# Last stage: loads in another order and exponentials grouped; prompt attention: both heads turned together

## The chip, the cores and the metric

The kernel runs on one core of a Trainium2 chip. The metric is the device time of one execution in microseconds. TensorE (PE in the rows) multiplies and transposes, VectorE (DVE) and ScalarE (ACT) work on what it leaves in PSUM, GpSimd (POOL) takes elementwise work on SBUF, and SyncE (SP) issues nearly all transfers between DRAM and SBUF. Each engine runs its own instructions in order; they meet through semaphores.

## The reference

One step of a two-layer decoder, for a prompt of 512 positions and for 8 samples of 4 new positions each over a past of 1024. All is float32. Layer A is a dilated sliding-window attention in three groups merged by their softmax denominators. Layer B has three branches with keys and values of their own: compressed blocks, the best selected blocks, a window.

```python
# layer A: for each group g, then merged over g by softmax of lse
s = q @ k.T * SCALE;  s = where(band, s, -inf)
o, lse = softmax(s) @ v, logsumexp(s)
# layer B, each sample (pool of pages through a page table)
hid   = silu(w1 . flatten(32 rows) + pe)         # compressed keys and values: w2 . hid
o_cmp = softmax(q . k_cmp) @ v_cmp               # its probabilities choose the 16 blocks
o_sel = softmax(q . k of the chosen blocks) @ v
o_win = softmax(q . k of the window) @ v
y = x + ((g0*o_cmp + g1*o_sel + g2*o_win) * silu(z)) @ w_out
```

## The kernel before

The program is a row of stages with a barrier between them: layer A (normalise, project, attention of the prompt, attention of the samples, output projection), then layer B the same way. Within a stage the order of each engine's work is written out by hand, and two stages are touched by the change.

**Attention of the prompt, layer A** (`attend_a_stage`). Sixteen steps: four query tiles by four pairs of heads. For each pair TensorE computes the scores of both heads (L585, L589) into four PSUM banks; VectorE adds the mask, writes the result to SBUF and keeps the least value (L669 to L675, "mask"); ScalarE takes the exponential and its sum (L642); VectorE inverts the sum (L680); GpSimd multiplies (L655); TensorE turns the 128 x 768 probabilities of one head with six transposes (L602); VectorE copies four of the six tiles to SBUF (L558) and ScalarE two (L560); TensorE multiplies by the values (L617). The steps are pipelined: in step s TensorE does the scores of s, the transposes of the first head of s-2, the values of s-3, and the transposes of the second head of s-2. There is one pair of banks for turned probabilities, so the second head's transposes wait for both copies of the first head. VectorE's order in a step is: mask of both heads, copy of the first head, one inversion, copy of the second head, the other inversion, and after every fourth step the product of a finished tile with the gate (L695, "merge"). The output of two tiles alternates between two banks.

**Samples, layer B** (`sample_b_stage`, the last stage). Two pieces of work are interleaved by a running number g, the quarter. The first piece compresses the pages of the 8 samples one after the other: transposes of pages (L1375), copies by VectorE and ScalarE, 16 products in a row into one bank (L1390), a silu on ScalarE (L1456), a small product (L1405). It takes 8 quarters a sample for 64 turns of pages, 72 quarters in all. The second piece is the attention of a pair of samples, 16 quarters each (a position i from 0 to 15), beginning at g = 20: transposes of keys of the window and of the selected pages (L2115, six units for i = 0 to 5), scores (L2130), the compressed scores (L2151, i = 4), the exponentials of the window (L2284, i = 3), of the compressed branch (L2290, i = 4) and of the selected branch (L2294, i = 10), the transposes of the probabilities (i = 12), the product with the values (L2174 to L2183, i = 14). Transposes of pages and of keys take turns on two PSUM banks, so each waits until the one before last has been copied. From g = 72 on the last pair's attention is interleaved with the output projection, 17 pieces (L2208): first the eight that use the second half of the output weights, then those of the first half. These weights overwrite the compression's weights and a page buffer.

The order of SP's queue is that of its issues in the code: `load_cmp(n)` loads the compressed branch's pages of sample n (8 transfers, L1550, two buffers), `load_keys(pair, units)` the keys of a pair (L2056 window, L2059 selected pages), `load_values(pair)` the values (L2069, L2070), which wait until the pair before has used its own. The page's number is read from a table in SBUF first (L2034). Behind the third pair's loads come the kept input (L2084) and the output weights (L2089 second half, L2092 first half).

ScalarE holds one table of functions; where the next function is in another table, the compiler puts an ACT_TABLE_LOAD in front. Exponential and silu are in different tables; copy and square do not ask for a load in this program.

Of the kernel before, what the change touches and what calls it, by code (L numbers as in the profile page):

```python
# [528 lines left out]
def attend_a_stage(S, QK, V, Z, T, oT, ring, tables):  # L529


    nc = S.nc
# [6 lines left out]
    with ExitStack() as ctx:  # L539
# [10 lines left out]
        SA, SB, TRA, TRB, OB = S.banks[0:2], S.banks[2:4], S.banks[4], S.banks[5], S.banks[6:8]  # L550
        ZB = [TRA, TRB, OB[0], OB[1]]

        def copy_out(engine, v, by_vector):
            engine.wait_ge(s_tr, v + 1)
            if v >= 4:
                engine.wait_ge(s_pv, v // 2 - 1)
            if by_vector:
                nc.vector.tensor_copy(pT[:, v % 4, 0:TILES, :], TRA[:, :].rearrange("p (c q) -> p c q", q=P)).then_inc(s_ev[0], 1)  # L558
            else:
                nc.scalar.activation(pT[:, v % 4, TILES:, :], TRB[:, 0:2 * P].rearrange("p (c q) -> p c q", q=P),  # L560
                                     ACT.Copy).then_inc(s_ev[1], 1)

        with S.block() as block:
# [8 lines left out]
            def _(pe):  # L572
# [20 lines left out]
                def turn(v):  # L593
                    pe.wait_ge(s_p, v + 1)
                    if v:
                        pe.wait_ge(s_ev[0], v)
                        pe.wait_ge(s_ev[1], v)
                    else:
                        pe.wait_ge(s_zc, 2)
                    for c in range(CH):  # L600
                        bank, at = (TRA, c) if c < TILES else (TRB, c - TILES)
                        ins = nc.tensor.transpose(bank[:, at * P:(at + 1) * P], probs[:, v % SLOTS, c * P:(c + 1) * P], ident)  # L602
                    ins.then_inc(s_tr, 1)

                def values(s):
                    t, j = divmod(s, HP)
                    for e in range(2):
                        pe.wait_ge(s_ev[e], 2 * (s + 1))
                    if s == 0:
                        pe.wait_ge(s_zc, TILES)  # L610
                    if j == 0 and t >= 2:
                        pe.wait_ge(s_fin, t - 1)
                    for c in range(CH):
                        g, kt = (0, c) if c < TILES else (c - TILES + 1, t)
                        for e in range(2):
                            h = 2 * j + e
                            ins = nc.tensor.matmul(OB[t % 2][e * DH:(e + 1) * DH, j * P:(j + 1) * P], V[:, g, kt, h * DH:(h + 1) * DH],  # L617
                                                   pT[:, (2 * s + e) % 4, c, :], start=(c == 0), stop=(c == CH - 1), skip_group_check=True)
# [39 lines left out]
            def _(dve):  # L658
# [4 lines left out]
                def mask(v):  # L663
# [3 lines left out]
                    if v >= SLOTS:  # L667
                        dve.wait_ge(s_tr, v - SLOTS + 1)
# [1886 lines left out]
```

## Time and profile before

| | us |
|---|---|
| median of 3 runs | 1436.12 (1435.59 to 1440.30) |
| the profiled execution | 1431.16 |
| its span, first to last instruction | 1429.4 |
| prompt attention of layer A | about 345 to 447 |
| last stage | about 1082 to 1429 |

Positions below are microseconds from the start of the span. A row of a timeline gives start, duration, engine, line, operation, what it writes and reads, and in brackets the time for which the engine stood idle before and what ended that. TensorE is busy for 89% of the span, the others for a third or less, but busy matmuls are partly waiting in the pipeline; the places where TensorE is idle say more.

### The profile page before, as it was taken

The page shows a single profiled execution, that of the slowest core. Times are in us where ns is not written, and L with a number is a line of the kernel's source. Part 1 is how long each engine was busy: PE and PEld are TensorE (multiplying, and loading weights), DVE is VectorE, ACT ScalarE, POOL GpSimd, SP SyncE. Part 2 cuts the span into 40 slices and gives each one's busy share as a digit, 9 for nine tenths or more (in the row PEclk, how much of TensorE's full clock was granted, in tenths as well). Part 3 has the DMA queues.
Part 4 walks back from the last instruction along what each step waited for, and adds up shares of the span by engine and source line. Part 5 has one row for each costly group of instructions (what it writes and reads, how often), then busy time and mean ns, then how long its engine had stood idle before and what let it go on. Part 6 is the DMA issues. An engine that isn't in the chain of part 4 may idle for free. (4 is left out here: it accounts for less than half of the span.)

```text
span 1429.4 us, 21435 instructions
## 1 busy us (share of the span) xinstructions
PE 1272.5 (89%) x7792; PEld 803.2 (56%) x7792; DVE 489.9 (34%) x1378; ACT 404.9 (28%) x958; POOL 362.3 (25%) x443
## 2 busy tenths in 40 slices
PE   3999999998886898889999998889998799999399
PEld 2576675764665762444444647655566567667144
DVE  1333332001675321223322102456773244534132
ACT  4111111112442210131211111456663244543100
POOL 1455553001774000026523100345441000000000
PEclk9999999999998998989999797689999899999699
DMA  6143333343104995132223531696454564553711
GB/s 221 55 179 119 127 149 149 129 177 79 37 2 113 278 265 141 36 143 89 88 88 97 208 63 30 218 336 238 148 207 157 154 203 141 181 182 109 180 24 63
DMA packets 88075, 200.26 MB, mean 140 GB/s; under 512 B 10131, under 2 KB 39235, under 8 KB 86563
## 3 DMA queue, kind: packets, MB, share of 16 engines
q1 hardware_dynamic: 87970, 198.89, 43.6%
q8 instruction: 63, 1.03, 0.3%
q14 instruction: 42, 0.34, 0.1%
HBM read 186.08 MB, written 75.37 MB: 183 GB/s over the span
## 5 line engine op out<-in xcount | busy, mean ns | idle before, releaser
L437 PE MATMUL bank<-la_region,la_hT 128*128 128x512 f32 x640 | 283.7, 600 | 1.6 <-PEq L162 1.6
L437 PEld LDWEIGHTS bank<-la_region,la_hT 128*128 128x128 f32 x640 | 165.7, 263 | 103.9 <-issue 61.9
L1183 PE MATMUL bank<-lb_region,lb_oT 128*128 128x512 f32 (+2 forms) x528 | 214.3, 568 | 1.6 <-PEq L162 1.6
L1183 PEld LDWEIGHTS bank<-lb_region,lb_oT 128*128 128x128 f32 (+1 forms) x528 | 99.4, 206 | 104.5 <-issue 104.2
L1390 PE MATMUL bank<-cs_chunks_turned,lb_region 128*128 128x252 f32 x512 | 126.3, 385 | 8.1 <-ACT cs_hidden L1456 8.0
L655 POOL TENSOR_SCALAR aa_probs<-aa_probs,aa_rec 128x768 f32<-128x768 f32 x32 | 70.2, 2205 | 137.8 <-DVE aa_rec L680 137.8
L1390 PEld LDWEIGHTS bank<-cs_chunks_turned,lb_region 128*128 128x128 f32 x512 | 92.1, 193 | 19.6 <-issue 7.2
L1759 POOL TENSOR_SCALAR ab_probs<-ab_probs,ab_rec,lb_gates 128x128 f32<-128x128 f32 (+3 forms) x128 | 75.9, 608 | 50.1 <-DVE ab_rec L1786 50.1
L2208 PE MATMUL bank<-lb_region,lb_oT 128*128 128x512 f32 x128 | 58.6, 610 | 22.6 <-DMA lb_region<-in_b_w_out 22.6
L1729 ACT ACTIVATE ab_probs<-ab_probs,ab_low 128x128 f32<-128x128 f32 (+3 forms) x128 | 70.4, 551 | 26.1 <-DVE ab_low L1780 25.9
L1445 DVE COPY cs_chunks_turned<-bank 64x512 f32<-64x512 f32 x64 | 43.7, 683 | 85.5 <-PE bank L1375 85.0
L485 POOL TENSOR_TENSOR pa_swapped<-pa_normed,pa_tables 128x256 f32<-128x256 f32 (+1 forms) x60 | 50.2, 855 | 77.3 <-DVE pa_normed L504 77.3
L1447 ACT ACTIVATE cs_chunks_turned<-bank 64x512 f32<-64x512 f32 x64 | 37.9, 593 | 95.7 <-PE bank L1375 95.0
L1684 PEld LDWEIGHTS bank<-consts,ab_probs 128*128 128x128 f32 (+1 forms) x384 | 43.9, 144 | 33.8 <-issue 19.5
L1684 PE MATMUL bank<-consts,ab_probs 128*128 128x128 f32 (+1 forms) x384 | 60.2, 298 | 2.5 <-POOL ab_probs L1752 1.5
L456 ACT ACTIVATE pa_squares<-bank 128x512 f32<-128x512 f32 (+1 forms) x30 | 16.0, 533 | 163.0 <-PE bank L437 155.4
L1487 POOL TENSOR_SCALAR cs_ms<-cs_ss 63x4 f32<-63x4 f32 x8 | 1.5, 186 | 229.3 <-DVE cs_ss L1498 229.3
L1780 DVE CUSTOM_DVE_ANT_0 ab_probs<-bank,consts 128x128 f32<-128x128 f32 (+3 forms) x128 | 56.1, 483 | 6.6 <-PE bank L1660 6.3
L2208 PEld LDWEIGHTS bank<-lb_region,lb_oT 128*128 128x128 f32 x128 | 24.2, 195 | 51.4 <-issue 50.3
L475 POOL TENSOR_TENSOR pa_rstd<-pa_mean_square,consts 128x8 f32<-128x8 f32 (+1 forms) x30 | 51.0, 1699 | 2.5
L1211 ACT ACTIVATE pb_squares<-bank 128x256 f32<-128x256 f32 (+3 forms) x25 | 10.6, 424 | 131.6 <-PE bank L1183 126.3
L1660 PE MATMUL bank<-lb_kT,lb_qp 64*128 64x128 f32 (+3 forms) x256 | 44.4, 484 | 3.0 <-DVE ab_low L1780 2.2
(312 smaller groups left out, 1807.0 us busy)
## 6 DMA issues: line engine op xcount, KB each, us to landing
la_region<-in_a_w_in SPq DMA_DIRECT2D x10, 2048.0 KB, 8.0
sb_sel_pages<-in_cache_nsa_paged SPq DMA_DIRECT2D x128, 128.0 KB, 2.4
out_new_dil_s<-in_cache_dil SPq DMA_DIRECT2D x8, 2032.0 KB, 12.5
lb_region<-in_b_w_in SPq DMA_DIRECT2D x7, 2048.0 KB, 7.8
sa_cache<-in_cache_dil SPq DMA_DIRECT2D x9, 1024.0 KB, 13.4
x<-in_cache_nsa_paged SPq DMA_DIRECT2D x32, 256.0 KB, 3.7
lb_region<-in_cache_nsa_paged SPq DMA_DIRECT2D x32, 256.0 KB, 3.9
sb_win_rows<-in_cache_nsa_win SPq DMA_DIRECT2D x16, 512.0 KB, 4.2
```

The lines of the kernel that those rows point to most:

```text
L437: ins = nc.tensor.matmul(U[u.v % 4][:, :], permuted(hT[:, k, :], u.g, u.t), W[:, u.c % 2, k, :], start=(k == 0), stop=(k == KC - 1))
L475: nc.gpsimd.tensor_tensor(rstd[:, i % 2, 0:u.H], ms[:, 0:u.H], S.const("half_power")[:, 0:u.H], ALU.pow).then_inc(s_rstd, 1)
L485: nc.gpsimd.tensor_tensor(o3[:, :, lo:lo + HALF], n3[:, :, HALF - lo:DH - lo], tab, ALU.mult).then_inc(s_sw, 1)
L655: nc.gpsimd.tensor_scalar(p, p, rec[:, v % SLOTS:v % SLOTS + 1], None, ALU.mult).then_inc(s_p, 1)
L1183: ins = nc.tensor.matmul(U[u.v % 3][0:u.R, 0:n], hT[:, k, u.t * P:u.t * P + u.R], W[:, u.c % 2, k, 0:n], start=(k == 0), stop=(k == KC - 1))
L1390: ins = nc.tensor.matmul(self.hid_bank[:, 0:KVH * nb], self.w1[:, kv, off, mm, :], self.chunksT[:, y % 2, :, mm, off:off + nb], start=(rm ...
L1660: nc.tensor.matmul(SC[u.i % 4][:, at:at + x.N], q, KT[part, x.br - 1, x.j, 0:x.N], start=True, stop=True, skip_group_check=True).then_inc( ...
L1684: ins = nc.tensor.transpose(TR[k2][0:x.rows, at:at + P], src[:, c * P:c * P + x.rows], ident)
L1729: nc.scalar.activation(row(u), row(u), ACT.Exp, bias=low[:, p, i:i + 1], scale=-1.0, accum_out=den[:, p, i:i + 1]).then_inc(s_e, 1)
L1759: nc.gpsimd.tensor_scalar(row(u), row(u), rec[:, x.b % 2, u.i:u.i + 1], gate, ALU.mult, ALU.mult).then_inc(s_p, 1)
L1780: nc.vector.tensor_tensor_reduce(row(u), SC[u.i % 4][:, at:at + x.N], S.const("causal")[:, (TILES - 1 - x.t) * P:], -SCALE, 3e38, ALU.add, ...
L2208: ins = nc.tensor.matmul(bank[:, :], oT[:, 4 * part + k, t * P:(t + 1) * P], W_out[:, 4 * part + k, half * 512:half * 512 + 512], start=(k ...
```

## The change

In the prompt attention the twelve transposes of a pair now stand together, with one signal at their end; VectorE has a bank for each head, ScalarE copies the rest of both heads at once (128 x 512), and the output has one bank for all tiles. VectorE's mask of the second head stands behind the copy of the first head's transposes, the inversions at the end of a step, and the merge at the beginning of a step instead of at its end. In the last stage the third sample's compressed pages are loaded behind three of six units of the first pair's keys, the fourth sample's ahead of the first pair's values, and the second half of the output weights ahead of the last pair's values. The exponential of the window moves from i = 3 to i = 4, next to that of the compressed branch, and behind each group of exponentials a silu of one element is added for as long as pages are compressed.

```diff
@@ attend_a_stage
-        SA, SB, TRA, TRB, OB = S.banks[0:2], S.banks[2:4], S.banks[4], S.banks[5], S.banks[6:8]
+        SA, SB, TRA, TRB, OB = S.banks[0:2], S.banks[2:4], S.banks[4:6], S.banks[6], S.banks[7]
...
+        def copy_first(s, e):
+            nc.vector.wait_ge(s_tr, s + 1)
+            if s >= 2:
+                nc.vector.wait_ge(s_pv, s - 1)
+            nc.vector.tensor_copy(pT[:, (2 * s + e) % 4, 0:TILES, :], TRA[e][:, :].rearrange("p (c q) -> p c q", q=P)).then_inc(s_ev[0], 1)
+
+        def copy_last(s):
+            nc.scalar.wait_ge(s_tr, s + 1)
...
+            nc.scalar.activation(pT[:, i:i + 2, TILES:, :], TRB[:, :].rearrange("p (e c q) -> p e c q", e=2, q=P),
+                                 ACT.Copy).then_inc(s_ev[1], 1)
...
+                def turn(s):
+                    if s:
+                        pe.wait_ge(s_ev[0], 2 * s)
+                        pe.wait_ge(s_ev[1], s)
...
+                    for e in range(2):
+                        v = 2 * s + e
+                        pe.wait_ge(s_p, v + 1)
+                        for c in range(CH):
+                            bank, at = (TRA[e], c) if c < TILES else (TRB, 2 * e + c - TILES)
+                            ins = nc.tensor.transpose(bank[:, at * P:(at + 1) * P], probs[:, v % SLOTS, c * P:(c + 1) * P], ident)
                     ins.then_inc(s_tr, 1)
...
                     if 2 <= s < NP + 2:
-                        turn(2 * (s - 2))
+                        turn(s - 2)
                     if s >= 3:
                         values(s - 3)
-                    if 2 <= s < NP + 2:
-                        turn(2 * (s - 2) + 1)
...
                 for s in range(NP + 4):
-                    if s < NP:
-                        mask(2 * s)
-                        mask(2 * s + 1)
+                    if s >= HP + 3 and (s - 3) % HP == 0:
+                        merge((s - 3) // HP - 1)
                     for e in range(2):
+                        if s < NP:
+                            mask(2 * s + e)
                         if 2 <= s < NP + 2:
-                            copy_out(dve, 2 * (s - 2) + e, True)
+                            copy_first(s - 2, e)
+                    for e in range(2):
                         if s < NP:
                             invert(2 * s + e)
@@ sample_b_stage, SP
                 load_cmp(1)
-                load_keys(0, range(NU))
+                load_keys(0, range(0, 3))
                 load_cmp(2)
+                load_keys(0, range(3, NU))
+                load_cmp(3)
                 load_values(0)
-                load_cmp(3)
...
-                    load_values(pair + 1)
-                    if pair == NPAIR - 2:
                         sp.wait_ge(C.m["tr"], 8 * NB)
                         for k2 in range(2):
                             sp.dma_start(W_out[k2 * DH:(k2 + 1) * DH, 4:8, :], w[1, k2]).then_inc(s_w[1], 16)
+                    load_values(pair + 1)
+                    if pair == NPAIR - 2:
                         sp.wait_ge(C.m["hm"], 2 * NB)
@@ sample_b_stage, ScalarE
-                    if i == 3:
+                    if i == 4:
                         act.wait_ge(m["lwin"], pair + 1)
                         nc.scalar.activation(pwin[:, :], pwin[:, :], ACT.Exp, bias=low[:, 2:3], scale=SCALE,
                                              accum_out=den[:, 2:3]).then_inc(m["ewin"], 1)
-                    if i == 4:
                         act.wait_ge(m["lcmp"], pair + 1)
...
+                        if g < C.quarters:
+                            nc.scalar.activation(idle[:, 1:2], idle[:, 0:1], ACT.Silu)
                     if i == 10:
...
+                        if g < C.quarters:
+                            nc.scalar.activation(idle[:, 1:2], idle[:, 0:1], ACT.Silu)
```

How this stands on the engines, at three places. Line numbers of the changed kernel are 5 to 13 higher.

TensorE, one step in the middle of the prompt attention (bank: PSUM; aa_probs: probabilities; aa_probs_turned: the same turned; la_v: values), before:

```order
L585 MATMUL bank<-la_qk 128x512 x2
L589 MATMUL bank<-la_qk 128x128 x4
L602 MATMUL bank<-consts,aa_probs 128x128 x6
L617 MATMUL bank<-aa_probs_turned,la_v 64x128 x12
L602 MATMUL bank<-consts,aa_probs 128x128 x6
```

The same step in the changed kernel:

```order
L590 MATMUL bank<-la_qk 128x512 x2
L594 MATMUL bank<-la_qk 128x128 x4
L609 MATMUL bank<-consts,aa_probs 128x128 x12
L624 MATMUL bank<-aa_probs_turned,la_v 64x128 x12
```

The second head's six transposes have moved from behind the values to ahead of them.

ScalarE, from the copy of the fourth key unit (i = 3) to the page copy of i = 5 in a pair that runs beside the compression (cs_hidden: the silu; sb_p_win, sb_p_cmp: exponentials; cs_chunks_turned, sb_keys_turned: copies that free a bank), before:

```order
L2264 ACTIVATE sb_keys_turned<-bank 128x512
L2284 ACT_TABLE_LOAD
L2284 ACTIVATE sb_p_win,sb_den<-sb_p_win,sb_low 128x544
L1456 ACT_TABLE_LOAD
L1456 ACTIVATE cs_hidden<-bank,lb_pe_hidden 128x4x63
L1447 ACTIVATE cs_chunks_turned<-bank 64x512
L2264 ACTIVATE sb_keys_turned<-bank 128x512
L2290 ACT_TABLE_LOAD
L2290 ACTIVATE sb_p_cmp,sb_den<-bank,sb_low 128x63
L1447 ACTIVATE cs_chunks_turned<-bank 64x512
```

The same stretch in the changed kernel:

```order
L2272 ACTIVATE sb_keys_turned<-bank 128x512
L1462 ACTIVATE cs_hidden<-bank,lb_pe_hidden 128x4x63
L1453 ACTIVATE cs_chunks_turned<-bank 64x512
L2272 ACTIVATE sb_keys_turned<-bank 128x512
L2293 ACT_TABLE_LOAD
L2293 ACTIVATE sb_p_win,sb_den<-sb_p_win,sb_low 128x544
L2298 ACTIVATE sb_p_cmp,sb_den<-bank,sb_low 128x63
L2301 ACT_TABLE_LOAD
L2301 ACTIVATE sb_idle<-sb_idle 1x1
L1453 ACTIVATE cs_chunks_turned<-bank 64x512
```

Two of three loads are left, and both stand between the second key copy and the page copy of i = 5.

SP, from the kept input on (x<-scratch_x), in two pieces, before; between them stand the other 17 transfers of the last pair's values:

```order
L2084 DMA x<-scratch_x 128x4096 [waits cs_tr]
L2034 TENSOR_LOAD page_table [waits sb_pv]
L2034 ISA x2
L2069 ISA
L2069 DMA sb_sel_pages<-in_cache_nsa_paged 128x256
```

```order
L2070 DMA sb_win_rows<-in_cache_nsa_win 128x4x256
L2089 DMA lb_region<-in_b_w_out 64x4x1024 [waits cs_tr]
L2089 DMA lb_region<-in_b_w_out 64x4x1024
L2092 DMA lb_region<-in_b_w_out 64x4x1024 [waits cs_hm]
L2092 DMA lb_region<-in_b_w_out 64x4x1024
```

In the changed kernel:

```order
L2092 DMA x<-scratch_x 128x4096 [waits cs_tr]
L2095 DMA lb_region<-in_b_w_out 64x4x1024 [waits cs_tr]
L2095 DMA lb_region<-in_b_w_out 64x4x1024
L2041 TENSOR_LOAD page_table [waits sb_pv]
L2041 ISA x2
L2076 ISA
L2076 DMA sb_sel_pages<-in_cache_nsa_paged 128x256
```

The two transfers of the weights' second half have moved ahead of the wait for the third pair's product (sb_pv); those of the first half stay behind the values.

## Rows read from the trace of the kernel before

**Rows 1.** First line of the page.

```profile
span 1429.4 us, 21435 instructions
```

**Rows 2.** Timeline of TensorE in the last stage: start, duration, what, idle before.

```profile
1114.09 1.87 PE L1390 MATMUL bank<-cs_chunks_turned,lb_region 128*128 128x252 f32 x8
1126.39 1.11 PE L1375 MATMUL bank<-consts,x 128*128 128x128 f32 x4 [10.44 <-DMA x<-in_cache_nsa_paged]
1127.29 2.77 PE L1390 MATMUL bank<-cs_chunks_turned,lb_region 128*128 128x252 f32 x8
...
1156.59 1.11 PE L1375 MATMUL bank<-consts,lb_region 128*128 128x128 f32 x4 [2.52 <-DMA lb_region<-in_cache_nsa_paged]
...
1183.63 0.60 PE L1375 MATMUL bank<-consts,x 128*128 128x128 f32 x4
...
1245.14 0.60 PE L1375 MATMUL bank<-consts,x 128*128 128x128 f32 x4
...
1308.47 1.94 PE L1390 MATMUL bank<-cs_chunks_turned,lb_region 128*128 128x252 f32 x8 [1.66 <-ACT cs_hidden L1456]
...
1354.63 5.25 PE L2208 MATMUL bank<-lb_region,lb_oT 128*128 128x512 f32 x8 [22.63 <-DMA lb_region<-in_b_w_out]
...
1378.75 13.98 PE L2208 MATMUL bank<-lb_region,lb_oT 128*128 128x512 f32 x32
```

**Rows 3.** List of waits, last stage: waiter, releaser, total us, times, longest.

```profile
PE bank L1390 <- ACT cs_hidden L1456: 8.0, 6, 1.9
```

**Rows 4.** Timeline of SP's issues in the last stage; duration covers all xN transfers.

```profile
1095.18 17.04 SPq L2059 DMA_DIRECT2D sb_sel_pages<-in_cache_nsa_paged  x16
1113.01 10.12 SPq L1550 DMA_DIRECT2D x<-in_cache_nsa_paged  x8
...
1163.98 10.08 SPq L1550 DMA_DIRECT2D x<-in_cache_nsa_paged  x8
...
1183.76 9.62 SPq L1550 DMA_DIRECT2D lb_region<-in_cache_nsa_paged  x8
1198.47 8.49 SPq L2069 DMA_DIRECT2D sb_sel_pages<-in_cache_nsa_paged  x8
...
1228.47 9.72 SPq L1550 DMA_DIRECT2D x<-in_cache_nsa_paged  x8
...
1320.59 8.45 SPq L2069 DMA_DIRECT2D sb_sel_pages<-in_cache_nsa_paged  x8
...
1339.17 1.29 SPq L2089 DMA_DIRECT2D lb_region<-in_b_w_out  x2
```

**Rows 5.** SP's own list of waits, last stage (L2183: end of a pair's product).

```profile
SPq L2034 <- PE bank L2183: 26.4, 3, 20.8
```

**Rows 6.** DMA issues, 1290 to 1360: KB each, median us from issue to landing.

```profile
lb_region<-in_b_w_out SPq DMA_DIRECT2D x4, 1024.0 KB, 16.8
```

**Rows 7.** Timeline of all engines about i = 4 of the second pair.

```profile
1218.61 1.28 ACT L1456 ACT_TABLE_LOAD   x1
...
1219.91 0.47 ACT L1456 ACTIVATE cs_hidden<-bank,lb_pe_hidden 128x252 f32<-128x252 f32 x1
...
1220.52 1.09 PE L1390 MATMUL bank<-cs_chunks_turned,lb_region 128*128 128x252 f32 x4 [1.86 <-ACT cs_hidden L1456]
...
1226.50 0.60 PE L2115 MATMUL bank<-consts,sb_sel_pages 128*128 128x128 f32 x4
```

**Rows 8.** Timeline of all engines, one step of the prompt attention.

```profile
373.63 0.85 PE L602 MATMUL bank<-consts,aa_probs 128*128 128x128 f32 x6 [0.93 <-DVE aa_probs_turned L558]
...
374.41 1.25 PE L585 MATMUL bank<-la_qk 64*128 64x512 f32 x4
...
376.15 0.69 DVE L669 CUSTOM_DVE_ANT_0 aa_probs<-bank,la_region 128x512 f32<-128x512 f32 x1 [0.88 <-PE bank L589]
...
378.51 0.69 DVE L558 COPY aa_probs_turned<-bank 128x512 f32<-128x512 f32 x1
...
379.30 0.85 PE L602 MATMUL bank<-consts,aa_probs 128*128 128x128 f32 x6 [0.93 <-DVE aa_probs_turned L558]
```

More of the change, by code:

```diff
@@ L549, in attend_a_stage @@
         s_ev = [S.sem("aa_copied_by_vector"), S.sem("aa_copied_by_scalar")]
-        SA, SB, TRA, TRB, OB = S.banks[0:2], S.banks[2:4], S.banks[4], S.banks[5], S.banks[6:8]
[L551 to L561, printed above, removed]
+        SA, SB, TRA, TRB, OB = S.banks[0:2], S.banks[2:4], S.banks[4:6], S.banks[6], S.banks[7]
+        ZB = [TRA[0], TRB, TRA[1], OB]
+        def copy_first(s, e):
[5 more added lines that the diff above has]
+            nc.scalar.wait_ge(s_tr, s + 1)
+            if s >= 2:
+                nc.scalar.wait_ge(s_pv, s - 1)
+            i = 2 * s % 4
+            nc.scalar.activation(pT[:, i:i + 2, TILES:, :], TRB[:, :].rearrange("p (e c q) -> p e c q", e=2, q=P),
+                                 ACT.Copy).then_inc(s_ev[1], 1)
         with S.block() as block:
@@ L591, in scores @@
                     ins.then_inc(s_sc, 1)
[L593 to L597, printed above, removed]
-                    else:
[L599 to L602, printed above, removed]
+                def turn(s):
+                    if s:
+                        pe.wait_ge(s_ev[0], 2 * s)
+                        pe.wait_ge(s_ev[1], s)
+                    else:
+                        pe.wait_ge(s_zc, 3)
+                    for e in range(2):
[4 more added lines that the diff above has]
+                            ins = nc.tensor.transpose(bank[:, at * P:(at + 1) * P], probs[:, v % SLOTS, c * P:(c + 1) * P], ident)
                     ins.then_inc(s_tr, 1)
@@ L606, in values @@
                     t, j = divmod(s, HP)
-                    for e in range(2):
-                        pe.wait_ge(s_ev[e], 2 * (s + 1))
+                    pe.wait_ge(s_ev[0], 2 * (s + 1))
+                    pe.wait_ge(s_ev[1], s + 1)
                     if s == 0:
                         pe.wait_ge(s_zc, TILES)
-                    if j == 0 and t >= 2:
-                        pe.wait_ge(s_fin, t - 1)
+                    if j == 0 and t:
+                        pe.wait_ge(s_fin, t)
                     for c in range(CH):
@@ L1955, in sample_b_stage @@
         y_rows = sb("sample_rows", [NS, D])
+        idle = sb("idle", [1, 2])
         s_k = [S.sem(f"sb_keys{u}") for u in range(NU)]
@@ L2267, in _ @@
             def _(act):
+                act.wait_ge(m["idle"], 1)
                 for g in range(NPOS):
@@ L2307, in _ @@
                 link = linker(dve, m["link"])
+                nc.vector.memset(idle[:, 0:1], 0.0).then_inc(m["idle"], 1)
                 link(nc.vector.memset(bmask[:, :], 0.0))
```

21 lines of the change are left out of this document (10 added, 11 removed).

## The prediction

> **What bounds the kernel now.** I read the page's first line, then the list of waits of the last stage, then SP's row of DMA issues against TensorE's timeline there, ScalarE around one pair of samples, and last one step of the prompt attention. The span is 1429.4 us [rows 1]; that execution took 1431.16, so 1.8 lies around the span, and it is 5.0 below the median of the runs, 1436.12. The sum is made against 1431.16 and then moved to the median.
>
> The last stage runs from about 1082 to the end. TensorE is its clock, with four kinds of holes. It waits 10.44 for the third sample's compressed pages, 2.52 for the fourth's, and 22.63 for the output weights [rows 2], and six times for the silu, 8.0 in all [rows 3]. After a long hole it restarts slowly: four transposes in 1.11 where 0.60 is usual and the products behind them in 2.77 instead of 1.87, eight output matmuls in 5.25 where 32 later ones take 13.98, so 3.50 per eight [rows 2].
>
> What the DMA waits rest on is SP. Sixteen selected pages cost it 17.04, so 1.07 each; eight compressed pages 9.6 to 10.1 [rows 4]. Between its first load and the second pair's values it is released by nothing it had waited for: its wait for the output product comes only three times, 20.8 of the 26.4 in the last [rows 5]. Until 1193.4 (1183.76 + 9.62) SP issues without a break. A load moved forward there moves another back.
>
> **Output weights.** Now they stand behind the last pair's values, which wait for the third pair's output product: SP starts at 1320.59, is through at 1339.17, and TensorE, ready at 1354.63 - 22.63 = 1332.0, starts at 1354.63. In the new order the second half (the one used first) waits only for the last page transposes, done before 1306.8 (1308.47 - 1.66) [rows 2]. With the 7.5 found below that is 1299.3; 1.3 to issue, and at most 16.8 to land, which was the time with all four pieces in flight [rows 6]: 1317.4, and TensorE comes at 1324.5. The wait goes whole, with the slow first projection: -22.63 - (5.25 - 3.50) = -24.4. Its cover is 7 us. What is late next would be the first half: values from 1313.1, 18.6 long, then 1.3 + 16.8 gives 1349.8. The ninth projection needs it; it now starts at 1378.75 + 3 x 3.5 = 1389.2, 34.6 after the first, so 1324.5 + 34.6 - 1.75 = 1357.3. Again 7 us of cover. If a piece took twice as long, some 10 us would return; nothing makes it better than -24.4.
>
> **Compressed pages.** After 4 selected pages instead of 16 SP begins the third sample's load at 1095.18 + 4.3 + 0.8 (the gap to 1113.01 now) = 1100.3, ends at 1110.4, and the data is there 3.3 later (1126.39 - 1123.13): 1113.7. TensorE comes at 1114.09 + 1.87 = 1115.96 [rows 2, 4]. So 10.4 goes, and 1.3 of slow restart (0.5 and 0.9 by the rows above, a little of it overlapped). Next, 0.8 + 12.8 of selected pages and 0.8 + 10.1: the fourth sample's last issue is at 1134.9, landed at 1138.2, wanted at 1156.59 - 2.52 - 11.7 = 1142.4. That wait goes too, with as much slow restart: TensorE is 15.6 early, 14.5 after the new wait of the next part.
>
> But then comes the fifth sample. Exactly the same loads stand ahead of it as now, SP had no slack there, so its issue still ends at 1163.98 + 10.08 = 1174.1 and lands at 1177.4. TensorE wants it at 1183.63 - 14.5 = 1169.1 and waits 8.3. What is kept is 1183.63 - 1177.4 = 6.2; the slow restart costs 1.3, and the silu wait of about 1.4 that followed here (8.0 over six) falls inside the new one: -6.3. The wait is moved, and more than half of the gain goes with it. From there SP's next loads: the second pair's values may start 6.3 earlier (1198.47 - 6.3 = 1192.2), but SP is busy until 1193.4 + 0.8 = 1194.2, so they move by 4.3, and the seventh sample's pages land at 1228.47 + 9.72 - 4.3 + 3.3 = 1237.2, wanted at 1245.14 - 7.0 = 1238.1. No wait, but only 0.9 of cover.
>
> **Exponentials and function tables.** A table load takes 1.28, and the next activation starts 0.02 after it [rows 7]. Before, each pair has six; after, four. The window's exponential no longer stands in front of the silu, so the hole of 1.86 before 1220.52 closes. In exchange both exponentials, the reload and a one-element silu (about 0.2, the read-out of an accumulator being 0.19) stand in one lump before the copy that frees a PSUM bank. From 1220.8 (the key copy, earlier by 1.9): load 1.28, window 0.94 and compressed 0.5 (estimates: twice and once the silu's 0.47), load 1.28, silu 0.2, copy 0.6 ends at 1225.7. The second key transposes that wait for that bank would come at 1226.50 - 1.9 = 1224.6 [rows 7]. So 1.1 is paid back, and 0.75 gained. At the selected branch, the load between exponential and silu is only placed one copy earlier on the same serial chain: the hole of 1.2 to 1.7 stays, plus 0.2 for the extra silu. Net -0.7 for each of pairs two and three (pair one's is lost in SP's wait), +0.2 at the last: with the 6.3, -7.5. Bounds for each pair: -1.9 (no payback) to +1.2.
>
> The Trainium skill prices a switch higher: "ScalarE: Activation LUTs", What ACT_TABLE_LOAD costs, counts some 1.28 for the load and 1.38 for a drain. By that the lump would be 2.8 longer and each pair 2.1 slower instead of 0.7 faster, the sum 5.6 worse. The trace agrees on the load (1.28) and shows no drain (0.02), so I leave it out.
>
> **Prompt attention.** A step is 5.67 (373.63 to 379.30) [rows 8], a loop: scores to first mask 1.74, two masks 2.36, copy of the first head to the next transposes 0.79, the second head's transposes 0.78. TensorE idles 0.93 of it, waiting for the copy. After: the first mask ends 1.74 + 1.18 = 2.92 after the scores' start, but both heads' transposes, 2 x 0.78 behind scores of 1.63 and a handover of 0.1, end at 3.3. Copy 0.6 to 0.7, second mask 1.18, handover 0.1: 5.25 to 5.3. Steps three to sixteen are 13 intervals: -0.4 x 13 = -5.2. Behind the last scores two steps remain, in each of which one wait of 0.9 for a copy goes: -1.7. The three merges, 1.1 each, now stand ahead of a step's masks, where VectorE waits 0.4 for the transposes and is idle before: nothing. One PSUM bank instead of two for the output makes the next tile's product wait for the merge, which ends some 3 us ahead of it. Sum -6.9. Bounds: TensorE's own work is 5.67 - 0.93 = 4.74 a step, so at best -0.93 x 13 - 1.7 = -13.8; at worst the longer transposes and the split masks add what they save and 0.2 a step, +2. I stay with -6.9. The sample stage's loads are issued behind this stage's end, so the shift carries through.
>
> **Sum.** -24.4 - 7.5 - 6.9 = -38.8: 1392.4 for the profiled execution, 1397 for the median.
>
> **Rivals.** (a) SP is no bound: the loads moved back have slack, and the gains of 10.4 and 2.5 stay. Then TensorE keeps the 14.5 instead of 6.3: 1389. For it: eight loads are there 3.3 behind their last issue, so the transfers themselves keep up. Against: no break in SP's issues until 1193.4. The Trainium skill's "DMA: Bandwidth & Descriptors", Issuing engines are not separate DMA queues, leans this way: issuing is usually small beside the transfer. Here eight issues take 10.1 us and the last data 3.3 more, so the trace contradicts it.
>
> (b) The prompt attention gains nothing: the copy that waits for both heads delays the second mask as much as it saves. For it: one signal for twelve transposes. Against: the two chains as added up. 1404.
>
> (c) The output weights are late all the same, because the two halves, the kept x and the values share the DMA engines: 8 to 13 us return, 1405 to 1410. For: 16.8 a piece; against: 7 us of cover at both places.
>
> (d) Slower than before: TensorE falls to 1.2 GHz in the prompt attention and stays. After each long hole of the last stage it ran at about half speed (1.11 for 0.60 [rows 2]). A step's 4.74 of work would take 9.5, +3.8 on 5.67; over all 13 steps +50 against -32 elsewhere, 1454. It decides from nine slow steps on. Against it: the waits get shorter (0.5 instead of 0.93 a step), and even behind a wait of 0.93 six transposes take 0.85 [rows 8], as fast per piece as the four in 0.60.
>
> **Chances.** Forecast 63% (its own range 1391 to 1402), (a) 9%, (b) 14%, (c) 10%, (d) 4%. What the timing can tell from no change is 0.3%, 4.3 us. Only (d) can be on the other side, 3% slower and 1% level; all else is faster, 96%. The range 1387 to 1410 takes in (a), (b) and (c); outside it I leave (d) and the ends of the others' own ranges.
>
> **What would show it.** In the changed profile: no wait before the first output projection, and its eight matmuls in 3.6; no wait at the third and fourth samples' first transposes; a new one of about 8 us at the fifth sample's, with SP's issue there at the same distance from the stage's start as now; six waits for silu turned into three of about 1.4, beside three of about 1.1 of key transposes for a ScalarE copy; steps of 5.3 in the prompt attention with TensorE idle 0.5 before the scores, not before transposes. It is wrong if the fifth sample's wait is missing, or if the weights are waited for.

## The result, and the profile after

The changed kernel takes 1400.99 us (median of 4 runs, 1389.85 to 1404.66), the kernel before 1438.21 in the same runs: ratio 0.9733, 95% interval 0.9678 to 0.9788. A second set, run with the last experiments, gives 1397.14 and 0.9729 (0.9697 to 0.9761). Predicted were 1397 against 1436.12, which is 0.9728. The median falls by 37.2 us in the first set, 38.8 were predicted.

The profiled execution is 41.3 us shorter than the one of before (span 1388.1 against 1429.4 [rows 1]); it was the quickest of its four runs, 1389.85, so the traces put the gain some 4 us higher than the medians do. By stages, each measured between the same instructions in both traces:

| | before | after | |
|---|---|---|---|
| to the first scores of the prompt attention | 347.1 | 345.7 | -1.4 |
| prompt attention, to the samples' first transposes | 101.9 | 92.4 | -9.5 |
| from there to SP's first load of the last stage (unchanged code) | 634.0 | 636.5 | +2.5 |
| last stage, from that load to the end | 346.5 | 313.5 | -32.9 |

TensorE's timeline of the last stage (columns as in [rows 2]): the first transposes of the third, fourth, fifth and seventh samples, a transpose of keys, a silu wait, and the first output products.

```profile
1107.72 0.60 PE L1381 MATMUL bank<-consts,x 128*128 128x128 f32 x4
...
1134.42 0.66 PE L1381 MATMUL bank<-consts,lb_region 128*128 128x128 f32 x4
...
1169.08 1.12 PE L1381 MATMUL bank<-consts,x 128*128 128x128 f32 x4 [8.29 <-DMA x<-in_cache_nsa_paged]
1169.99 2.82 PE L1396 MATMUL bank<-cs_chunks_turned,lb_region 128*128 128x252 f32 x8
...
1210.71 0.63 PE L2123 MATMUL bank<-consts,sb_sel_pages 128*128 128x128 f32 x4 [0.72 <-ACT cs_chunks_turned L1453]
...
1229.20 0.60 PE L1381 MATMUL bank<-consts,x 128*128 128x128 f32 x4
1231.23 1.94 PE L1396 MATMUL bank<-cs_chunks_turned,lb_region 128*128 128x252 f32 x8 [1.44 <-ACT cs_hidden L1462]
...
1314.96 3.60 PE L2216 MATMUL bank<-lb_region,lb_oT 128*128 128x512 f32 x8
```

The waits of 10.44, 2.52 and 22.63 [rows 2] are gone; one of 8.29 is new, at the fifth sample, and behind it TensorE restarts as slowly as it did behind the old ones.

SP's issues, before (the stage's first load) and after:

```profile
1082.95 10.15 SPq L1550 DMA_DIRECT2D lb_region<-in_cache_nsa_paged  x8
```

```profile
1074.56 10.16 SPq L1556 DMA_DIRECT2D lb_region<-in_cache_nsa_paged  x8
...
1091.31 9.69 SPq L1556 DMA_DIRECT2D x<-in_cache_nsa_paged  x8
...
1115.48 9.65 SPq L1556 DMA_DIRECT2D lb_region<-in_cache_nsa_paged  x8
...
1155.99 10.12 SPq L1556 DMA_DIRECT2D x<-in_cache_nsa_paged  x8
...
1288.05 1.31 SPq L2095 DMA_DIRECT2D lb_region<-in_b_w_out  x2
...
1303.72 8.51 SPq L2076 DMA_DIRECT2D sb_sel_pages<-in_cache_nsa_paged  x8
```

The fifth sample's load begins 81.4 us behind the first one (1155.99 - 1074.56), before 81.0 (1163.98 [rows 4] - 1082.95): the third and fourth samples' loads moved forward, but everything that stood ahead of the fifth one still does, and so it stayed where it was.

ScalarE at i = 4 of the second pair (answers to [rows 7]):

```profile
1205.41 0.60 ACT L2272 ACTIVATE sb_keys_turned<-bank 128x512 f32<-128x512 f32 x1 [1.13 <-PE bank L2123]
1206.02 1.28 ACT L2293 ACT_TABLE_LOAD   x1
1207.32 0.75 ACT L2293 ACTIVATE sb_p_win<-sb_p_win,sb_low 128x544 f32<-128x544 f32 x1
...
1208.06 0.29 ACT L2298 ACTIVATE sb_p_cmp<-bank,sb_low 128x63 f32<-128x63 f32 x1
...
1208.46 1.28 ACT L2301 ACT_TABLE_LOAD   x1
1209.76 0.20 ACT L2301 ACTIVATE sb_idle<-sb_idle 1x1 f32<-1x1 f32 x1
1209.97 0.59 ACT L1453 ACTIVATE cs_chunks_turned<-bank 64x512 f32<-64x512 f32 x1
```

The row of instructions between the key copy and the page copy (the "lump" of the prediction) stands as predicted; the page copy ends at 1210.56 and the key transposes that wait for its bank follow at 1210.71.

One step of the prompt attention, all engines (answers to [rows 8]); the last two rows are from the next step:

```profile
374.80 1.25 PE L590 MATMUL bank<-la_qk 64*128 64x512 f32 x4 [0.47 <-DVE aa_low L680]
...
376.43 1.53 PE L609 MATMUL bank<-consts,aa_probs 128*128 128x128 f32 x12
...
378.00 0.69 DVE L558 COPY aa_probs_turned<-bank 128x512 f32<-128x512 f32 x1 [0.21 <-PE bank L609]
378.60 0.68 DVE L674 CUSTOM_DVE_ANT_0 aa_probs<-bank,la_region 128x512 f32<-128x512 f32 x1
...
379.89 1.25 PE L590 MATMUL bank<-la_qk 64*128 64x512 f32 x4 [0.47 <-DVE aa_low L680]
...
381.01 1.11 DVE L690 TENSOR_TENSOR la_hT<-bank,la_hT 128x512 f32<-128x512 f32 x1
...
385.50 1.25 PE L590 MATMUL bank<-la_qk 64*128 64x512 f32 x4 [1.00 <-DVE aa_low L680]
```

A step is 5.09 (379.89 - 374.80) instead of 5.67; the one that contains a merge (L690) is 5.61.

### The profile page after: what moved, and what is told of

Its sections match the earlier page's. It is cut to its first block and busy times, and to the rows that moved or that the text cites. A ratio compares the mean times of both kernels' runs of the same rounds, so it can differ in the third digit from the quotient of the medians.

```text
span 1388.1 us, 21391 instructions
## 1 busy us (share of the span) xinstructions
PE 1265.0 (91%) x7792; PEld 798.8 (58%) x7792; DVE 491.9 (35%) x1379; ACT 396.9 (29%) x942; POOL 362.6 (26%) x443
## 5 line engine op out<-in xcount | busy, mean ns | idle before, releaser
L660 POOL TENSOR_SCALAR aa_probs<-aa_probs,aa_rec 128x768 f32<-128x768 f32 x32 | 70.2, 2205 | 131.0 <-DVE aa_rec L685 130.9
L1453 ACT ACTIVATE cs_chunks_turned<-bank 64x512 f32<-64x512 f32 x64 | 38.0, 593 | 94.5 <-PE bank L1381 93.9
L1281 DVE TENSOR_REDUCE pb_square_sum<-pb_squares 128x4 f32<-128x256 f32 (+3 forms) x25 | 11.7, 468 | 91.2 <-ACT pb_squares L1217 91.2
```

Of the source, the lines that this page charges most:

```text
L660: nc.gpsimd.tensor_scalar(p, p, rec[:, v % SLOTS:v % SLOTS + 1], None, ALU.mult).then_inc(s_p, 1)
```

## The experiments

Each kernel is the changed one with the edit shown below; the edits are abridged, with words in parentheses for code that is left out. "Last stage" runs from SP's first load there to the end, in the profiled execution. A profile shows one execution, so its times by stage have no interval.

| | ratio to before (95%) | last stage |
|---|---|---|
| changed kernel | 0.9733 (0.9678 to 0.9788) | 313.5 |
| weights back | 0.9898 (0.9861 to 0.9934) | 341.8 |
| compressed pages back | 0.9782 (0.9741 to 0.9823) | 319.1 |
| prompt attention back | 0.9779 (0.9729 to 0.9829) | 313.5 |
| exponentials back | 0.9759 (0.9717 to 0.9801) | 317.9 |
| fifth sample's pages earlier | 0.9709 (0.9674 to 0.9744) | 313.9 |
| fifth's and seventh's earlier | 0.9665 (0.9621 to 0.9710) | 305.1 |
| fixed page numbers | 0.9645 (0.9605 to 0.9686) | 304.3 |
| no early reload, merge moved | 0.9683 (0.9639 to 0.9726) | 313.6 |
| combined | 0.9614 (0.9585 to 0.9643) | 304.4 |
| changed kernel again | 0.9729 (0.9697 to 0.9761) | 313.5 |
| combined, weights earlier still | 0.9624 (0.9590 to 0.9659) | 302.5 |

The intervals of the single undone parts, weights apart, overlap that of the changed kernel; for these the traces decide.

**Weights back.**

```diff
-                        (wait for the last page transposes; load W_out, second half)
                     load_values(pair + 1)
+                    if pair == NPAIR - 2: (the same wait and load)
```

> The changed kernel with one part undone: the second half of the output weights is loaded behind the last pair's values again. Theory (place in SP's queue): SP takes up the values about 11 us before TensorE comes to the first output products, needs 18.6 for them, then 1.3 and 16.8 for the weights, so TensorE waits 22 to 24 us there again and restarts slowly (5.2 instead of 3.6 for the first eight); the last stage, 313.5 us in the changed kernel from the first issue of the second sample's pages to the end, becomes 336 to 339. Rival (weights were late only because the rest was late): the wait is under 15 us, last stage under 330.

TensorE's timeline at the first output products:

```profile
1345.61 6.48 PE L2216 MATMUL bank<-lb_region,lb_oT 128*128 128x512 f32 x8 [23.45 <-DMA lb_region<-in_b_w_out]
```

The wait is back in its full size, the rival's "under 15" falls. The stage is 28.2 longer, more than the 22.5 to 25.5 expected: 23.5 of wait, 2.9 of restart (6.48 instead of 3.60), and 1.7 between the first and second pairs' first key transposes (70.2 instead of 68.6), where the restart behind the fifth sample's wait lasted longer. So the restart is the unsteady part of such a price, and the granted clock shows why. In the first 5 us behind the fifth sample's wait it was 0.72 in the changed kernel and 0.50 here (1.00 is 2.4 GHz, 0.50 is 1.2 GHz). Behind the waits for pages of 5.9 us and more, eight products took 2.76 to 2.82 in four profiles, at 0.72 or 0.73, and 3.56 or 3.57 in five, at 0.50; the longest of these waits, 10.4, has the quicker restart and the shortest the slower. Up to the second pair's keys, the slower restart costs about 1.6 (19.0 from the fifth sample's first transposes instead of 17.4).

**Compressed pages back.**

```diff
-                load_keys(0, range(0, 3));  load_cmp(2)
-                load_keys(0, range(3, NU)); load_cmp(3); load_values(0)
+                load_keys(0, range(NU)); load_cmp(2)
+                load_values(0);          load_cmp(3)
```

> The changed kernel with one part undone: the third and fourth samples' compressed pages are loaded in the old places. Theory (SP's queue has no slack until the second pair's values, so the loads moved forward only shifted the wait): waits of about 10.4 and 2.5 us at the third and fourth samples' first transposes return, the 8.3 at the fifth sample's goes; last stage 313.5 + 6 to 7.5 = 319.5 to 321. Rival (the wait at the fifth sample has another cause, SP is no bound): the 8.3 stays beside the other two, last stage 327 to 329.

```profile
1127.19 1.11 PE L1381 MATMUL bank<-consts,x 128*128 128x128 f32 x4 [10.01 <-DMA x<-in_cache_nsa_paged]
...
1157.30 0.66 PE L1381 MATMUL bank<-consts,lb_region 128*128 128x128 f32 x4 [0.85 <-DMA lb_region<-in_cache_nsa_paged]
```

The third sample's wait returns with 10.0, the fourth's is only 0.85 here, the fifth's 8.3 is gone; the stage is 5.6 longer, just under the 6 to 7.5 expected. Some 1.6 of the 5.6 is the slower restart (3.57 for eight products behind the third sample's wait), so the reorder by itself is worth 4 to 5.6, not the 10.4 and 2.5 that one sees vanish.

**Prompt attention back.** The whole stage function as before.

> The changed kernel with one part undone: the prompt attention as before, the last stage as changed. Theory (the loop got shorter): a step is 5.67 again instead of 5.09, from the first scores to the first transposes of the samples 100.3 us where the clock is full at the start (101.9 if it dips there), against 92.4 in the changed kernel; the whole +7 to +9.5. Rival (the saving was the clock at the stage's start, 0.5 for some us in the one profile): the steps are 5.67, but the stage is no more than 96 when the clock is full. The last stage stays 313 to 314 in both.

Steps of 5.67 again, the stage 105.1, the last stage 313.5, unchanged to 0.1. The stage is longer than the 100.3 to 101.9 expected: the granted clock was down to 0.50 at the start (360 to 365) and once more behind the last scores, where 24 products with the values took 2.83 instead of 1.53. With its old attention the kernel took 101.9 and 105.1 in two profiles, with the new one 92.4 to 97.3 in eight. The full clock at the start that the rival (no more than 96) supposes is in neither profile of the old order, so read the part behind the start: from the fifth scores to the stage's end the eight profiles of the new order take 73.5 each, the two of the old one 80.3 and 81.8. So the gain is not the clock of the start, and the rival falls, but its mechanism is real, see "changed kernel again". The whole lost less than the stage: 0.9779 against 0.9733 is 6.6 us, where 7 to 9.5 were expected, and the intervals overlap (see the last section).

**Exponentials back.**

```diff
-                    if i == 4:    # window exponential
+                    if i == 3:
...
-                        if g < C.quarters: (one-element Silu)       # twice
```

> The changed kernel with one part undone: exponentials at i = 3, 4 and 10 as before, without the one-element silu. Theory: six waits for the silu, 7 to 8 us, and no wait of key transposes for ScalarE's page copy: last stage 313.5 + 1.5 to 3 = 315 to 316.5; one pair's period (first key transposes of the second pair to those of the third, 60.36) grows by 0.7 to 1.2. Rival (the lump costs as much as it saves): last stage and period within 0.4 of the changed kernel's. Beyond what the times can tell; the trace decides.

A pair's period is read between its first key transposes and those of the next pair. Second to third pair, in the kernel before, the changed one and this one:

```profile
1201.11 0.63 PE L2115 MATMUL bank<-consts,sb_win_rows 128*128 128x128 f32 x4 [0.60 <-DVE lb_oT L2413]
...
1262.62 0.63 PE L2115 MATMUL bank<-consts,sb_win_rows 128*128 128x128 f32 x4 [0.60 <-DVE lb_oT L2413]
```

```profile
1186.52 0.63 PE L2123 MATMUL bank<-consts,sb_win_rows 128*128 128x128 f32 x4 [0.60 <-DVE lb_oT L2426]
...
1246.88 0.63 PE L2123 MATMUL bank<-consts,sb_win_rows 128*128 128x128 f32 x4 [0.60 <-DVE lb_oT L2426]
```

```profile
1202.75 0.63 PE L2123 MATMUL bank<-consts,sb_win_rows 128*128 128x128 f32 x4 [0.60 <-DVE lb_oT L2423]
...
1264.25 0.63 PE L2123 MATMUL bank<-consts,sb_win_rows 128*128 128x128 f32 x4 [0.60 <-DVE lb_oT L2423]
```

61.51, 60.36, 61.50: the grouping gives 1.15 for a pair, and nothing else of the change does. Of the waits, those of keys for a page copy are gone as expected, and those for the silu are 8.9 in all, over the 7 to 8 expected. The stage grew by 4.3, more than the 3 expected: 0.7 up to the fifth sample, 2.3 in the periods of the second and third pairs, and 1.3 because the restart behind the fifth sample's wait was again longer (3.57 for the first eight products, against 2.82).

**Fifth sample's pages earlier; fifth's and seventh's earlier.** The second edit; the first does it for `pair == 0` alone.

```diff
-                    load_keys(pair + 1, range(0, 4))
                     load_cmp(2 * pair + 4)
+                    load_keys(pair + 1, range(0, 4))
```

> The changed kernel with the fifth sample's compressed pages loaded ahead of the second pair's first keys instead of behind them (both are needed later than that). Theory (SP issues without a break, so what is moved forward moves the rest back): the 8.3 us wait at the fifth sample goes, but the seventh sample's pages are issued where they were, land about 1229.3 on the changed kernel's clock and are wanted at 1229.2 - 9.6 = 1219.6: a new wait of 9 to 10 us there, last stage 313.5 within 1.5. Rival (one shortfall, slack behind it): no wait at the seventh sample, last stage 303 to 305.

> As the kernel with the fifth sample's pages moved, and the seventh sample's moved ahead of the third pair's first keys in the same way. Theory: the seventh's land at 1204.9 + 9.7 + 3.3 = 1217.9, wanted at 1219.6; the eighth's at 1249, wanted at 1253.8; keys and weights keep 3 us and more. No wait for pages but the second sample's 2.2: last stage 303 to 305, the whole 9 to 10 us below the changed kernel. Rival (it moves once more, to the eighth sample, to the keys or to the weights): last stage 309 to 314.

TensorE's timeline with the first edit, at the seventh sample:

```profile
1229.35 1.11 PE L1381 MATMUL bank<-consts,x 128*128 128x128 f32 x4 [7.22 <-DMA x<-in_cache_nsa_paged]
```

TensorE's list of waits with both, its longest entries (waiter, releaser, total, times, longest):

```profile
PE bank L1396 <- ACT cs_hidden L1462: 5.2, 5, 1.9
PE bank L2123 <- ACT cs_chunks_turned L1453: 2.2, 3, 0.7
PE bank L1381 <- DMA lb_region<-in_cache_nsa_paged: 1.7, 1, 1.7
```

One load moved: the wait goes to the seventh sample, 7.2 long (under the 9 to 10 expected) and with the slower restart behind it (3.56), and the stage gains nothing, 313.9. Both moved: of the waits for pages only the second sample's is left, and the stage is 8.5 shorter. The same edit is worth 0 or 8.5, depending on whether the next load in the queue has been cared for.

**Fixed page numbers.** Reads pages n * 8 + pg instead of those of the table, so y of the samples differs.

```diff
-    page = sp.value_load(S.page_table[...]);  src = cache[0, DynSlice(page, 1)]
+    at = n * NPAGES + pg;                     src = cache[0, at:at + 1]
```

> The changed kernel with page numbers fixed in the last stage's own loads, that is without the reading of the page table: other pages are read, with the same number of transfers and bytes in the same order, and outputs differ. Theory (SP's issuing is what the fifth sample waits for): an issue takes 0.6 us, as the window's do, instead of 1.07 to 1.27; eight take about 5, so all pages are there early, the 8.3 and most of the second sample's 2.2 go, last stage 300 to 304. Rival (the transfers themselves are the bound): issues are shorter, but the data is no earlier, the wait at the fifth sample is 7 to 9, last stage 311 to 314.

SP's issues, the second and fifth samples' pages:

```profile
1077.93 5.10 SPq L2053 DMA_DIRECT2D lb_region<-in_cache_nsa_paged  x8
...
1137.31 5.08 SPq L2053 DMA_DIRECT2D x<-in_cache_nsa_paged  x8
```

0.64 an issue instead of 1.27, the same bytes, no wait for pages anywhere, the stage 9.3 shorter (304.3, at the upper end of the 300 to 304 expected). The rival falls. Half of what SP spends on a page here is the reading of its number together with the address made from it; the run does not tell these two apart.

**No early reload, merge moved.**

```diff
-                        if g < C.quarters: (one-element Silu)       # twice
...
-                    if s >= HP + 3 and (s - 3) % HP == 0: merge((s - 3) // HP - 1)   # ahead of the masks
+                    if s == NP + 3: merge(TILES - 1)                                 # the last one stays
+                    if HP + 2 <= s < NP + 2 and (s - 2) % HP == 0: merge((s - 2) // HP - 1)  # behind copy_first
```

> The changed kernel with two small edits, each to be read in its own stage. First, without the one-element silu, so the table comes back only in front of the next real silu. Theory: the reload hides in ScalarE's idle time (1.1 us before the silu of i = 7), the lump is 1.5 shorter, the three waits of 0.72 of key transposes for ScalarE's copy go, silu waits stay as they are (3.7 in all): the period of a pair 60.36 - 0.7 to 1.0. Rival (the early reload is what closes the stall): new silu waits of 1 to 1.9 in each pair, period 61 to 62. Second, in the prompt attention the merge stands behind VectorE's second copy instead of ahead of the next step's mask. Theory (the merge delays a mask that the next scores wait for): the two steps of 5.61 become 5.1 to 5.3. Rival (another cause): they stay 5.6. The whole: within 4 us of the changed kernel, not to be told by times.

The first key transposes of the second and third pairs, then ScalarE from the compressed exponential of the second pair to the next silu:

```profile
1199.40 0.63 PE L2125 MATMUL bank<-consts,sb_win_rows 128*128 128x128 f32 x4 [0.60 <-DVE lb_oT L2424]
...
1258.82 0.63 PE L2125 MATMUL bank<-consts,sb_win_rows 128*128 128x128 f32 x4 [0.60 <-DVE lb_oT L2424]
```

```profile
1221.13 0.19 ACT L2300 ACTIVATION_READ_ACCUMULATOR sb_p_cmp<-bank,sb_low 128x1 f32 x1
1221.35 0.59 ACT L1455 ACTIVATE cs_chunks_turned<-bank 64x512 f32<-64x512 f32 x1
...
1229.24 0.59 ACT L1455 ACTIVATE cs_chunks_turned<-bank 64x512 f32<-64x512 f32 x1 [2.89 <-PE bank L1383]
1229.85 1.28 ACT L1464 ACT_TABLE_LOAD   x1
1231.15 0.47 ACT L1464 ACTIVATE cs_hidden<-bank,lb_pe_hidden 128x252 f32<-128x252 f32 x1
```

The load stands in time in which ScalarE would have waited for TensorE, no new silu wait appears (3.3 in all), and the period is 59.42, another 0.94 less: the wait of 0.72 of the key transposes is gone, and the silu wait at i = 10 is back from 1.44 to 1.22. So grouping the exponentials gains, and bringing the table back early loses. All merge steps are 5.08 or 5.09: the merge had delayed the next step's first mask. The last stage, 313.6, does not show the gain: that of the first pair went into a longer wait at the fifth sample (10.0), whose first transposes even came 0.6 later behind SP's first load (95.1 instead of 94.5), and the 1.9 of the other two pairs went into this and the slower restart (3.57 for eight products, 1.4 up to the next keys).

**Combined, and the changed kernel again.**

```diff
-                load_values(0)
+                load_values(0, (0,)); load_cmp(4); load_values(0, (1,))
...
-                    load_cmp(2 * pair + 4)
...
-                    load_values(pair + 1)
+                    load_values(pair + 1, (0,)); load_cmp(2 * pair + 6); load_values(pair + 1, (1,))
```

together with the two edits of the kernel ahead of it.

> The changed kernel with what the runs so far point to: the fifth and seventh samples' compressed pages are loaded between the two halves of the pair's values (instead of behind the next pair's keys), no one-element silu, and the merge behind VectorE's second copy. Theory (the gains are in different places and add up): last stage 305.1 - 3 x 0.94 = 302 to 303 against 313.5, all steps of the prompt attention 5.1, the whole some 12 us below the changed kernel: ratio to the kernel before 0.962 to 0.967 where the changed kernel has 0.973. Rival (they share a limit, SP or the DMA engines, so the pages or the weights are waited for again): a wait of over 2 us at a sample's first transposes beside the second's, or at the first output product, and a last stage of 306 or more.

> The changed kernel once more, beside the combined one on the same chip: last stage 313 to 316, ratio to the kernel before 0.968 to 0.979. If the clock at the start of the prompt attention is chance, its second to fourth steps may differ by up to 4 us from the 4.46, 5.09 and 5.08 of the first profile, with nothing changed; if it belongs to the kernel, they are the same.

Combined 0.9614 (0.9585 to 0.9643) against 0.9729 (0.9697 to 0.9761) on the same chip: 1384.99 and 1397.14 us. TensorE's timeline shows what kept the stage at 304.4 instead of 302 to 303:

```profile
1311.50 3.67 PE L2221 MATMUL bank<-lb_region,lb_oT 128*128 128x512 f32 x8 [1.66 <-DMA lb_region<-in_b_w_out]
```

The changed kernel again: the granted clock at the start of the prompt attention (columns: stretch, its length, each engine's busy time, granted clock, DMA share, GB/s), first profile and second:

```profile
355.00:360.00 5.00, 3.07 (x26) 2.37 (x25) 3.89 (x13) 2.46 (x6) 4.00 (x2) 1.00 1.01 260
360.00:365.00 5.00, 4.54 (x50) 3.66 (x50) 3.75 (x15) 2.45 (x6) 4.39 (x2) 1.00 0.10 34
```

```profile
355.00:360.00 5.00, 3.92 (x22) 3.15 (x20) 2.41 (x8) 1.79 (x5) 3.69 (x2) 0.66 1.00 259
360.00:365.00 5.00, 4.16 (x23) 3.58 (x24) 3.33 (x13) 1.34 (x3) 3.44 (x2) 0.71 0.04 13
```

The same program, a stage of 92.4 and of 95.6; the second to fourth steps take 4.46, 5.09, 5.08 and 4.47, 6.69, 6.66.

**Combined, weights earlier still.**

```diff
+                    if pair == NPAIR - 2: (wait for the last page transposes; load W_out, second half)
                     load_keys(pair + 1, range(4, NU))
```

in place of the load behind the kept x.

> The combined kernel with the second half of the output weights moved once more, ahead of the last pair's last eight selected pages and of the kept x. Theory (in the combined kernel SP comes to the weights only at the end of the last keys, and their 2 MB share the DMA engines with the 2 MB of x issued just ahead): the wait of 1.66 before the first output product goes, last stage 304.4 - 1.7 = 302 to 303. Rival (the DMA engines are the limit there, and something else is late instead): a wait of 1 us or more at the last pair's keys, its values, or the first additions of x, and a last stage of 304 or more. Too little for the times: the trace decides.

The wait is gone and the stage is 302.5, as expected; in the times (0.9624, 0.9590 to 0.9659) it is level with the combined kernel.

## Why the prediction was right, point by point

**Output weights, -24.4.** Measured 22.63 + (5.25 - 3.60) = 24.3. The cover was larger than the 7 worked out. DMA issues of 1286 to 1295, the second half alone:

```profile
lb_region<-in_b_w_out SPq DMA_DIRECT2D x2, 1024.0 KB, 13.1
```

So it had landed by about 1289.4 + 13.1 = 1302.5, and TensorE came at 1314.96, some 12 later; the 16.8 of the old order [rows 6] was with four pieces in flight. The first half has as much: issued by 1323.7, landed 12.3 later at 1336.0, first used by the ninth projection at about 1347.9. Rival (c) falls.

**Compressed pages, -6.3.** The wait of 8.3 was predicted and is 8.29; the fifth sample's first transposes come 94.5 behind SP's first load instead of 100.7 (1169.08 - 1074.56, 1183.63 [rows 2] - 1082.95). Undone by itself it costs 5.6, 1.6 of which is a slower restart. The sum prices every slow restart alike, at 1.3; that the new one behind the fifth sample's wait was of the quicker kind in this profile (2.82, against 2.77 behind the old wait) was luck. Rival (a) is refuted twice: moving the fifth's load cures the fifth sample, and with the same transfers but cheaper issues no page is late. The cover of 0.9 at the seventh sample was in fact about nothing: no wait in this profile, but 0.25 in the second one of the same kernel. The Trainium skill's "DMA: Bandwidth & Descriptors", Issuing engines are not separate DMA queues, counts issuing as usually small beside the transfer. That does not hold for these loads: eight issues with a page number read from a table took 10.1, and the last data came 3.3 later.

**Exponentials, -0.7 a pair.** The mechanism was right, the size was off. The prediction's own terms, 0.75 gained and 0.2 paid at the selected branch, make -0.55. The new wait of keys is 0.72, not 1.1, because the lump was priced 0.3 too long (window and compressed exponential with their accumulators 1.13, 1207.32 to 1208.45, estimated 1.44); the waits at i = 10 grew by 0.2 as said (1.44 and 1.87, before 1.22 and 1.66). The period fell by 1.15: the listed waits give 0.9 of it (1.86 - 0.72 - 0.22), the rest stays open. That an early reload is a loss by itself was not seen: the prediction set it against the old order as a whole. By the Trainium skill's "ScalarE: Activation LUTs", What ACT_TABLE_LOAD costs, a switch takes about 2.66 us, which would have made each pair slower. The trace does not bear it out: the period fell, and the activation begins 0.02 behind the load here too.

**Prompt attention, -6.9.** From the fourth scores to the stage's end, free of the start's clock in the changed kernel's profile: 78.5 instead of 85.9, so -7.4. The step came to 5.09, not 5.25 to 5.3 (the terms as listed add up to 5.18 to 5.28): twelve transposes stand in a row in 1.46, not 2 x 0.78, and the next mask begins 0.60 behind the start of the copy, the lower end of its 0.6 to 0.7. Against it, the "nothing" for the merges was wrong: 0.53 in each of two steps, since VectorE is idle ahead of a mask for 0.54, less than the merge's 1.1; and the end behind the last scores gave 1.4, not 1.7. The other 2 of the 9.5 lie in the steps ahead of that, 5.44 and 6.26 for the second and third before, 4.46 and 5.09 in the changed kernel's first profile: the clock granted there was 1.00 in the latter, and the changed kernel's second profile has 6.69 for the third. Rival (b) falls. Rival (d) happens, but for the first steps alone, in the old order and the new, and costs up to 5 us, not 50.

**Sum.** -38.8 predicted, of which -31.9 from the last stage (measured -32.9) and -6.9 from the attention (-9.5, of which 2 are chance). What the prediction put at nothing is the stage behind the attention ("the shift carries through"): in this profile it took 2.7 longer than before, in others up to 11.6 (last section). So that the medians fell by 37.2, so near to 38.8, is in part luck: gains a little larger than predicted against a longer stage behind them.

## What to carry to other kernels

A queue that issues without a break has to be added up like an engine: a load moved forward moves the next one back, so look for the first consumer behind the moved load, and move that one too. A reload or a merge placed "early" is only early if its engine had nothing on the path at that time; put it into a hole, even if that hole is later. Read small edits from the stage they are in, between the same instructions, not from the whole time, and then look whether the stage behind it kept the gain.

## What was not expected of the hardware

With the same code and the same waits of 2.6 to 2.8 us ahead of the second and third steps' scores, the start of the prompt attention is granted the full clock (2.4 GHz) in one profile and partly the lower level (1.2 GHz) in the next: 92.4 to 97.3 us for the stage in eight profiles. The restart behind a wait for pages is of two kinds in the same way.

And the samples' attention of layer A, the next stage, has a DMA share of about 1 in its loads; its code is untouched and its loads are issued in the same order. From its first transposes to the first output product it took 120.9 and 121.0 us in the two profiles with the old prompt attention (the kernel before, and prompt attention back), and 123.2 to 132.5 in the eleven with the new one: a spread larger than three of the four parts of this change. Behind the old attention TensorE waits for loads once in front of its products with the values there, 3.2 and 2.7 us; behind the new one mostly twice, 4.0 to 8.1 in all. Whether the new attention brings this about, and how, no run here shows; that the two lowest of thirteen values are the two of the old attention speaks against chance alone. If it does, this stage gives back 2 us or more of the 7 to 10 that the prompt attention gains, in some executions all of it.
